# Sparse-index stage of a two-block transformer kernel: turns and index products moved inside other products, waits moved, and the root and layer norm written with fewer operations

## The reference, cut to what matters

```
for i in range(DEPTH):          # i = 0: fox, i = 1: dsa
    x = _layer_norm(DN_ALPHA * x + mixers[i](x), ln_g[i], ln_b[i], LN_EPS)

# _layer_norm
xc = xf - mean(xf);  var = mean(xc * xc);  xc * rsqrt(var + eps) * g + b

# _dsa_mixer, one block of 128 queries
q, ckv, kr, qi, ki, wi, gate = _split(x @ w_in, ...)
ckv = _rms_norm(ckv, ...)                   # q, kr, qi, ki get rotary tables
isc = relu(einsum('bqhd,bsd->bqhs', qi_b, ki) * di ** -0.5)      # index scores
isc = einsum('bqhs,bqh->bqs', isc, wi_b)
_, idx = lax.top_k(isc, 64)                 # causal, 64 keys per query
p = softmax(q_full . kv_lat[idx]);  o = (p . ckv[idx]) . w_uv
return (silu(gate) * o) @ w_out
```

## Time and profile before

| what | before |
|---|---|
| median of 3 runs | 1311.47 us (1310.27 to 1311.47) |
| span of the profiled execution | 1310.3 us |
| instructions in it | 16491 |
| TensorE busy | 1270.2 us, 97% |
| VectorE busy | 873.9 us, 67% |
| ScalarE busy | 613.6 us, 47% |
| mean granted TensorE clock | 0.992 of full |

### The profile page before, as it was taken

How to read it: one execution, slowest core, us unless ns; L and a number is a source line. 1 busy time by engine, 2 the same in 40 slices (tenths; PEclk the granted TensorE clock), 3 DMA queues, 4 the chain that set the end, 5 groups by cost and what they waited for, 6 DMA issues and landing times.

```text
span 1310.3 us, 16491 instructions
## 1 busy us (share of the span) xinstructions
PE 1270.2 (97%) x6717; PEld 1077.6 (82%) x6717; DVE 873.9 (67%) x1312; ACT 613.6 (47%) x839; POOL 24.2 (2%) x37
## 2 busy tenths in 40 slices
PE   6999999989999999999999999999999999999997
PEld 5888888988788888878888886778888899988876
DVE  6655557885755556685657569856555567566896
ACT  6444346435434445444435357654444344544461
POOL 2000000100000000000000000000000000000000
PEclk9999999999999999999999989999999999999999
DMA  9655545443555556565665440065666686446401
GB/s 329 207 182 187 186 162 185 142 155 129 183 184 185 188 192 186 166 193 170 217 224 169 159 161 1 1 200 187 191 193 193 130 217 172 150 130 211 176 2 65
DMA packets 158812, 218.17 MB, mean 167 GB/s; under 512 B 8257, under 2 KB 110993, under 8 KB 158737
## 3 DMA queue, kind: packets, MB, share of 16 engines
q1 hardware_dynamic: 156880, 212.56, 51.2%
q0 software_dynamic: 1376, 3.71, 0.9%
q10 hardware_dynamic: 480, 0.85, 0.2%
HBM read 216.04 MB, written 1.05 MB: 166 GB/s over the span
## 4 chain that ended last, share of the span: by engine, by line
PE 82%; DVE 11%; issue 3%; ACT 2%; SPq 1%; DMA 1%; DVEq 0%
PE PS L686 23%; PE PS L689 23%; PE PS L687 23%; DVE wlo L2050 2%; PE PS L823 1%; PE PS L721 1%; PE PS L722 1%; ACT whi L1523 1%; PE PS L706 1%; PE PS L1300 1%; DVE arena L2639 1%; PE PS L728 1%; PE PS L1016 1%; SPq L591 1%; DVE XL L2090 1%
## 5 line engine op out<-in xcount | busy, mean ns | idle before, releaser
L2050 DVE TENSOR_TENSOR wlo<-raw,whi 128x2048 fp32r<-128x2048 f32 (+4 forms) x206 | 457.4, 2230 | 122.6 <-ACT whi L1523 121.8
L1523 ACT ACTIVATE whi<-raw 128x2048 fp32r<-128x2048 f32 (+4 forms) x206 | 381.4, 1863 | 63.4 <-DMA raw<-in_fox_w_in_dram 33.1
L686 PE MATMUL PS<-whi,XL 128*128 128x512 f32 (+3 forms) x992 | 385.8, 390 | 8.9 <-DVE scr L2152 3.8
L687 PE MATMUL PS<-wlo,XH 128*128 128x512 f32 (+3 forms) x992 | 379.8, 384 | 0.0
L689 PE MATMUL PS<-whi,XH 128*128 128x512 f32 (+3 forms) x992 | 265.0, 384 | 0.0
L686 PEld LDWEIGHTS PS<-whi,XL 128*128 128x128 f32 x992 | 187.3, 189 | 45.1 <-DVE scr L2152 4.9
L689 PEld LDWEIGHTS PS<-whi,XH 128*128 128x128 f32 x992 | 185.5, 190 | 35.5
L687 PEld LDWEIGHTS PS<-wlo,XH 128*128 128x128 f32 x992 | 187.4, 189 | 32.9
L1577 ACT ACTIVATE scr<-PS,rn 128x256 f32<-128x256 f32 x88 | 41.7, 474 | 225.2 <-PE PS L689 223.9
L686 PE MATMUL PS<-whi,GL 128*128 128x512 f32 x320 | 125.4, 392 | 0.0
L687 PE MATMUL PS<-wlo,GH 128*128 128x512 f32 x320 | 124.6, 389 | 0.0
(11 more groups left out here) (387 smaller groups left out, 1339.2 us busy)
## 6 DMA issues: line engine op xcount, KB each, us to landing
raw<-in_ffn_w_in_dram SPq DMA_DIRECT2D x174, 512.0 KB, 5.0
raw<-in_ffn_w_out_dram SPq DMA_DIRECT2D x88, 512.0 KB, 4.9
raw<-in_fox_w_in_dram SPq DMA_DIRECT2D x24, 512.0 KB, 7.9
raw<-in_a_w_in_dram SPq DMA_DIRECT2D x16, 512.0 KB, 4.6
raw<-in_dsa_w_in_dram SPq DMA_DIRECT2D x16, 512.0 KB, 6.0
raw<-in_kv_w_dram SPq DMA_DIRECT2D x12, 512.0 KB, 4.2
raw<-in_fox_w_in_dram SPq DMA_DIRECT2D x12, 344.0 KB, 5.0
raw<-in_a_w_out_dram SPq DMA_DIRECT2D x8, 512.0 KB, 4.9
```

The source lines that it names most:

```text
L686: mm(o, xl, wh, start=start and i == 0, stop=False, skip_group_check=True)
L687: mm(o, xh, wl, start=False, stop=False, skip_group_check=True)
L1523: A(whi[:, p % SLOTS, 0:n], raw[:, p % SLOTS, 0:n], ACT.Copy).then_inc(hi_done, 1)
L2050: V.tensor_tensor(wlo[:, p % SLOTS, 0:n], raw[:, p % SLOTS, 0:n], whi[:, p % SLOTS, 0:n].bitcast(F32), ALU.subtract).then_inc(lo_done, 1)
```

## The change

The edits, in program order on each engine.

- TensorE: the turn of the first tile of "dsa" stood after the whole fox output product; it now stands inside it, after part i = 2 of tile t = 1.
- TensorE: in chunk 2, tile t = 0, second piece, the products with `whi` come first and wait for `hi_done` only, and those with `wlo` come last, behind a wait for `lo_done`.
- TensorE: the wait for `ki_ready` and the first four index products stood ahead of chunk 4; the first two now come after its tile m = 0, the other two after m = 1.
- TensorE: the wait for the eviction of `dv3` stood ahead of chunk 5; it now stands ahead of the first turn of the softmax weights, after tile m = 1 of chunk 5.
- VectorE: the low part of piece first+9 and the eviction of chunk 3 are now ahead of the eviction of `kr`.
- VectorE: in both attentions `second_of_pt(.., 2)` is ahead of `silu_second`.
- VectorE: `root` begins with one operation on the integer view in place of a shift and a multiply-add, and where w is 1 the two products `y*y*s` are one operation with `s` as a per-partition scalar.
- VectorE: the shift of the layer norm is one operation in place of two.

```diff
--- before.py
+++ after.py
@@ turn_first (TensorE, attend_four) @@
                 def turn_first():
+                    if stage == "dsa":
+                        pe.wait_ge(side_act, looks(side_no["dv3"], "act"))
                     turn_p(0)
@@ end of attend_four @@
                 for i in range(4):
                     out_part(name, 1, i)
+                    if i == 2 and stage == "fox":
+                        for w in range(2):
+                            turn_h("dsa", 0, w)
@@ chunks 0 to 2 of dsa (TensorE) @@
-            for w in range(2):
-                turn_h("dsa", 0, w)
...
+                        if (t, c, i) == (0, 2, 1):
+                            pe.wait_ge(hi_done, end)
+                            for k in range(4):
+                                mm(o, XL[:, 4 + k, 0:P], wh[:, k, :], start=False, stop=False, skip_group_check=True)
+                            for k in range(4):
+                                mm(o, XH[:, 4 + k, 0:P], wh[:, k, :], start=False, stop=False, skip_group_check=True)
+                            pe.wait_ge(lo_done, end)
+                            for k in range(4):
+                                last = mm(o, XH[:, 4 + k, 0:P], wl[:, k, :], start=False, stop=k == 3, skip_group_check=True)
+                            last.then_inc(chunk_ps, 1)
+                            continue
@@ index products (TensorE) @@
-            pe.wait_ge(ki_ready, 1)
...
-            for i in range(4):
-                index_products(i)
-            chunk("dsa", 4)
+            def first_index():
+
+                pe.wait_ge(ki_ready, 1)
+                index_products(0)
+                index_products(1)
+
+            def next_index():
+
+                index_products(2)
+                index_products(3)
+
+            chunk("dsa", 4, None, {0: first_index, 1: next_index})
@@ ahead of chunk 5 (TensorE) @@
-                pe.wait_ge(side_act, looks(side_no["dv3"], "act"))
                 chunk("dsa", 5, None, between)
@@ root (VectorE) @@
+                def scaled_square():
+
+                    if w == 1:
+                        link(V.scalar_tensor_tensor(out=v, in0=y, scalar=s, in1=y, op0=ALU.mult, op1=ALU.mult))
+                    else:
+                        link(V.tensor_tensor(v, y, y, ALU.mult))
+                        link(V.tensor_tensor(v, v, s, ALU.mult))
-                link(V.tensor_scalar(y.bitcast(U32), v.bitcast(U32), 1, None, ALU.logical_shift_right))
-                V.tensor_scalar(v, v, -ROOT_A * ROOT_L, None, ALU.mult).then_inc(dve_step, 1)
+                V.tensor_scalar(y.bitcast(I32), v.bitcast(I32), -0.5, float(0x5F1FFFF9), ALU.mult, ALU.add).then_inc(dve_step, 1)
                 steps[0] += 1
-                link(V.tensor_scalar(y.bitcast(I32), y.bitcast(I32), -1.0, float(0x5F1FFFF9), ALU.mult, ALU.add))
-                link(V.tensor_tensor(t_, y, y, ALU.mult))
-                link(V.tensor_tensor(t_, t_, v, ALU.mult))
...
+                link(V.tensor_scalar(s, v, -ROOT_A * ROOT_L, None, ALU.mult))
+                scaled_square()
+                link(V.scalar_tensor_tensor(out=y, in0=v, scalar=ROOT_C, in1=y, op0=ALU.add, op1=ALU.mult))
+                scaled_square()
@@ layer_norm (VectorE) @@
-                link(V.tensor_tensor(shift, lns[:, 2 * t:2 * t + 1], lns[:, 2 * t + 1:2 * t + 2], ALU.add))
-                V.tensor_scalar(shift, shift, -1.0 / D, None, ALU.mult).then_inc(for_act, 1)
+                V.tensor_scalar(shift, lns[:, 2 * t:2 * t + 1], lns[:, 2 * t + 1:2 * t + 2], -1.0 / D, ALU.add, ALU.mult)\
+                    .then_inc(for_act, 1)
@@ attention, fox and dsa alike (VectorE) @@
             silu_first("dsa", 5, 4, 4)
+            second_of_pt("dsa", 2)
             silu_second("dsa", 5, 4)
-            second_of_pt("dsa", 2)
@@ after the keys of dsa (VectorE) @@
-            split_to(first + 9)
+            split_to(first + 10)
+            dve.wait_ge(used, chunk_end("dsa", 3))
+            V.tensor_copy(xs[:, 1, 512:1024], bank_of("dsa", 3, 1)).then_inc(chunk_dve, 1)
             o = side("kr")
             dve.wait_ge(pads_ready, 6)
             V.tensor_copy(d_krT[0:32, :], o[0:32, 0:T]).then_inc(side_dve, 1)
-            dve.wait_ge(used, chunk_end("dsa", 3))
-            V.tensor_copy(xs[:, 1, 512:1024], bank_of("dsa", 3, 1)).then_inc(chunk_dve, 1)
-            split_to(first + 10)
```

More of the change, by code:

```diff
@@ L1416, in _ @@
                                 turn_h("dsa", 1, w)
+                        wh, wl = parts_n(end - 2 + i, 4, n)
+                        pe.wait_ge(x_ready, x_at("dsa", t, 4 * i + 3))
+                        o = PS[:, dsa_bank(c, t), 0:n]
+                        if (t, c, i) == (0, 2, 1):
[9 more added lines that the diff above has]
+                            continue
                         if t == 0:
                             pe.wait_ge(lo_done, end - 1 + i)
[L1419 to L1423, removed]
+                        last = product(o, [(XH[:, 4 * i + k, t * P:t * P + P], XL[:, 4 * i + k, t * P:t * P + P],
+                                            wh[:, k, :], wl[:, k, :]) for k in range(4)], start=i == 0, stop=i == 1)
                         if t == 1:
                             last.then_inc(used, 1)
-                    if t == 0:
+                    if t == 0 and c < 2:
                         last.then_inc(chunk_ps, 1)
@@ L2058, in root @@
             def root(name, w, to=rr):
-                y, v, t_ = ry[:, 0:w], rv[:, 0:w], rt[:, 0:w]
-                link(V.tensor_scalar(y.bitcast(U32), v.bitcast(U32), 1, None, ALU.logical_shift_right))
-                V.tensor_scalar(v, v, -ROOT_A * ROOT_L, None, ALU.mult).then_inc(dve_step, 1)
-                steps[0] += 1
-                link(V.tensor_scalar(y.bitcast(I32), y.bitcast(I32), -1.0, float(0x5F1FFFF9), ALU.mult, ALU.add))
-                link(V.tensor_tensor(t_, y, y, ALU.mult))
-                link(V.tensor_tensor(t_, t_, v, ALU.mult))
[L2068 to L2072, removed]
+                y, v, s = ry[:, 0:w], rv[:, 0:w], rt[:, 0:w]
+                def scaled_square():
[5 more added lines that the diff above has]
+                V.tensor_scalar(y.bitcast(I32), v.bitcast(I32), -0.5, float(0x5F1FFFF9), ALU.mult, ALU.add).then_inc(dve_step, 1)
+                steps[0] += 1
+                link(V.tensor_scalar(s, v, -ROOT_A * ROOT_L, None, ALU.mult))
+                scaled_square()
+                link(V.scalar_tensor_tensor(out=y, in0=v, scalar=ROOT_C, in1=y, op0=ALU.add, op1=ALU.mult))
+                scaled_square()
+                link(V.scalar_tensor_tensor(out=s, in0=v, scalar=10 * ROOT_B / 3, in1=v, op0=ALU.add, op1=ALU.mult))
+                V.scalar_tensor_tensor(out=to[:, 0:w], in0=s, scalar=5 * ROOT_B * ROOT_B, in1=y, op0=ALU.add, op1=ALU.mult)\
                     .then_inc(root_out, 1)
@@ L2782, in _ @@
             silu_first("fox", 8, 4, 2)
+            second_of_pt("fox", 2)
             silu_second("fox", 8, 4)
-            second_of_pt("fox", 2)
             raw_second("fox")
```

## The result

| | before | after |
|---|---|---|
| median | 1311.47 us (1310.27 to 1314.44, 4 runs) | 1304.17 us (1303.24 to 1304.96, 4 runs) |
| ratio after / before | | 0.9945, 95% interval 0.9929 to 0.996 |
| span of the profiled execution | 1310.3 us | 1302.1 us |
| instructions | 16491 | 16461 |

The change makes the kernel faster by about 7 us, 0.55%. In the two profiled executions the gain is 8.2 us of span. The time of the changed kernel's profiled run is 1303.86 us, 1.8 us above its span: a run's time has something around the span that the numbers of before did not show.

What follows compares the result with a forecast made beforehand. TensorE, 97% busy, was taken as the bound, so only its waits could be won, with VectorE the bound from 1250 to 1277 us. Terms of 6.4 us off 1310.3 gave 1303.9, forecast as 1304.2 us; 8-in-10 range 1301.9 to 1307.2.

Steps and rivals of the forecast that it cites:

- Turn (forecast 1.1) and low part (1.7): Fox output product and chunk 2: TensorE's 1.1 us wait behind the turn and 1.7 us wait for a low part go.
- `second_of_pt` in fox: Fox attention: the copy passes a 0.6 us operation, removing a TensorE wait of 0.3 to 0.4 us; gain 0.3 us.
- Index products and VectorE's order: Around chunk 4: VectorE could reach the index scores 1.9 us sooner, but the relu limits the gain to 0.9 us.
- `dv3`: Chunk 5: TensorE starts 1.2 us sooner, but VectorE is full, so the wait returns at the chunk's end; gain 0.
- `second_of_pt` in dsa: Dsa attention: the copy passes `silu_second`, 0.6 us, and TensorE waits for it, so all 0.6 us is gained.
- The end: After the last product: layer norm loses one dependent operation and the root three, 4 x 0.19 = 0.8 us.
- rival B: Roots and end: a removed operation is worth 0.07 us, not a link; 1305.1 us, chance 0.05.
- Roots elsewhere: Sixteen roots lose the shift; five stand before a longer TensorE wait for VectorE, 5 x 0.2 = 1.0 us.
- rival C: Keys root: the operation that took 1.79 us may fall where nobody waits, gaining more; 1302.7 us, chance 0.12.
- Rival D: From 1180 us VectorE bounds everything, so edits to order do nothing; 1307.7 to 1308.5 us, chance 0.07.
- rival A: Low part and index terms: late weight loads delay ScalarE's high parts, losing 1.7 and 0.9; 1306.5 us, chance 0.13.
- Rival E: Before the index products: piece first+9 lands late, stopping VectorE and TensorE; slower by over 2.6 us, chance 0.03.

Runs made afterwards that it cites:

- experiment 2: Changed kernel with the turn of dsa put back: 1305.31 us; with chunk 2's old product order: 1305.11 us; with both put back: 1306.61 us.
- experiment 1: Kernel before with only the new root and layer norm shift: 1308.26 us; changed kernel with the old root and shift: 1306.81 us.
- experiment 5: Changed kernel with index products and VectorE's order both put back: 1305.01 us; with VectorE's old order alone: 1306.41 us.
- experiment 6: Changed kernel with the first two index products between the two pieces of chunk 4's tile m = 0: 1303.03 us, ratio 0.9929.
- experiment 7: Changed kernel with the root's y*y*s as two operations for w = 1 also: 1304.45 us.

## Why the prediction was right, and where it was not

The forecast of 1304.2 us stands beside 1304.17, but the terms are not as good as that, and two errors hide each other. The terms sum to 6.4 us; the medians differ by 7.3 and the spans by 8.2. And the sum was taken from the span of before, 1310.3 us, as if it were a run's time, where the changed kernel's runs are 1.7 to 1.8 us above their spans. From the median of before, 6.4 us would have given 1305.1 us. That the last digits agree is luck.

- **Turn (forecast 1.1) and low part (1.7): nearly right in sum, wrong in reason.** Before to after this part gains 3.4 us; 2.7 of it go with the two edits (experiment 2), and the rest with the norm, whose shorter chain the order makes superfluous (experiment 1). The steps that failed are "With the turn 2.7 us earlier all this moves forward by about that" and "Either alone covers a wait of 1.7 us". VectorE moved forward by 1.5 us, for it lost the rest to a weight that had not landed, and TensorE, which the step left where it was, moved by 1.3. The early turn covers 0.1 to 0.2 of the wait; it is the later need that takes it away.
- **`second_of_pt` in fox (0.3): 0.2.** The wait of 0.4 us at L1016 is in the kernel with root and norm only and not in the others, but from TensorE's 5201st matmul to the first product of the fox output it takes 91.84 us before, 91.83 us with root and norm only and 91.68 us after. It was not put back by itself.
- **Index products and VectorE's order (0.9): right, with the reason.** It measures 0.8 us by experiment 5 and 0.9 between the traces. The step that set it, that the relu comes last and takes 1.0 of the 1.9 us, is seen as VectorE's 1.08 us of idle time, and experiment 6 took it away.
- **`dv3` (0): right.** Both signs showed: 0.28 + 0.17 us for the scaling, 0.79 for the copy, together the 1.2 us.
- **`second_of_pt` in dsa (0.6): 0.4.** "All of the 0.6 is on the path" was too much; the wait grows by 0.6, the end moves by 0.4.
- **The end (0.8): 0.6.** The forecast took the plain operation's price for the one with a scalar per partition and named the other as what would make it wrong. It costs 0.06 us more, in two places of each root and in the norm's new shift: 4 x 0.195 - 3 x 0.06 = 0.6. Two plain operations against one gave 0.13 us each time in experiment 7, and the pitch of a dependent one is 0.195 us. The Trainium skill, "Perfetto Trace Analysis", section Optimizing Scalar/DVE Operations, gives about 60 ns as the fixed cost of a VectorE operation on SBUF. Here a dependent operation that is left out gives back more than that: the measured link decides, and rival B is out.
- **Roots elsewhere (1.0): mis-sized, about 2.6.** The term counted five waits of one link each. Seven waits of TensorE shrink. Six do by about 0.2 us each, together 1.3: those at the head root, the two feed-forward starts and the attention root, and two that the forecast did not have, near 246 us (1.03 us before, 0.82 after) and near 821 us (1.11 and 0.95). The keys root gave not a link but 1.35 us, by the time from L1138 or L1143 to L823 on TensorE (13.64 us before, 12.29 after). All seven are within 0.05 us of before with order only, and within 0.05 us of the changed kernel with root and norm only. The keys root is rival C, and it came true beside the forecast rather than in its place.

TensorE's waits of the changed kernel from 280 to 880 us:

```profile
PE PS L737 <- DVE xs L2435: 2.2, 1, 2.2
PE PS L686 <- DVE scr L2179: 1.3, 2, 0.7
...
PE PS L686 <- DVE wlo L2071: 0.5, 1, 0.5
```

With the measured sizes: 3.4 + 0.2 + 0.9 + 0 + 0.4 + 0.6 + 2.6 = 8.1 us, of 8.2. That so little is left is luck again: the 2.0 us that before lost in the first 57 us, and what the changed kernel gave back by chance at other places, 1.3 us of it around 246 us, happen to cancel. The medians, 7.3 us apart with an interval of 5.2 to 9.3, agree with the sum and cannot test it closer.

Rival D did not happen. Of rival A the mechanism did: ScalarE's high part waited 1.0 us for its load, and it ate half of VectorE's head start. It cost no time, since the low part was needed late. Rival E, a late low part of piece first+9, did not happen in the change, but TensorE's stop at that place is real: take VectorE's half of the edit away, and it is 1.4 us. The scores came at 1222.98 us, 7.2 sooner than 1230.16 and not the 5 forecast: 2.9 of it lie ahead of the fox output, with the chance of above in them, and 4.3 behind it.

## What to carry to other kernels

An edit that moves both engines forward shortens the wait between them only by the difference; ask of each edit how far it moves either one, and whether a load then comes last. A moved wait has to be priced at the next place where the same two engines meet, and the two halves of a reordering on two engines have to be made together, for one half can be worse than none. Compare a stretch between two instructions and not only run times: here it told apart edits of 0.4 us where a run's time could not. And before two traces are subtracted, look where the granted clock differs between them.

## What the runs showed of the hardware

- On VectorE a dependent 128x1 operation cost 0.195 us from start to start, and one with a scalar per partition 0.26 (experiment 7).
- An operation of 128x16 on VectorE took 1.79 and 1.84 us instead of 0.18 in both kernels with the old root, together with the one issued beside it, and never with the new. With the one operation that the new root saves there it cost TensorE 1.35 us. The cause is open; five more instructions ahead did not bring it back.
- The first 1150 us of kernels that are nearly alike there differ by up to 3 us. TensorE's granted clock was 0.50 to 0.52 at 27 us in one trace of fourteen, and at 246 us in four; 3 us of it held 9 matmuls against 15, and 16 against 26.
